# A second MLP product by Strassen: block sums and low parts of both operands on VectorE

## The reference

```python
a = jnp.square(jax.nn.relu(jnp.einsum('btd,df->btf', rmsnorm(h, ln2), w_ff1)))
return h + jnp.einsum('btf,fd->btd', a, w_ff2)
...
y_prompt = rmsnorm(yp, ln_f)
```

## Time and profile before

| | us |
|---|---|
| median of 3 runs | 1367.07 (1362.38 to 1369.3) |
| the profiled execution | 1365.83 |
| its span in the trace | 1363.9 |
| TensorE busy | 1287.0 (94%) |
| VectorE busy | 832.2 (61%) |
| GpSimd busy | 654.5 (48%) |
| ScalarE busy | 593.2 (43%) |

### The profile page before, as it was taken

One profiled execution on the slowest core, in us unless ns is written; L12 is line 12 of the kernel. 1 busy time (PEld: TensorE's weight loads), 2 busy tenths in 40 slices (PEclk: granted clock), 3 DMA queues, 4 the chain that ended last, 5 costly groups with the idle time before them and its releaser, 6 DMA issues.

```text
span 1363.9 us, 25942 instructions
## 1 busy us (share of the span) xinstructions
PE 1287.0 (94%) x10008; PEld 1190.0 (87%) x10008; DVE 832.2 (61%) x1678; ACT 593.2 (43%) x1099; POOL 654.5 (48%) x588
## 2 busy tenths in 40 slices
PE   5999999999998999999999999999979998986898
PEld 5859999995666899789999999999979998986798
DVE  6368997669874222148634334335578677598955
ACT  6445888638765223236443333334112323321334
POOL 5434984433312113121567667675448477385500
PEclk9999999999999999999999999999999998997899
DMA  6430124210011866871333233233801502402003
GB/s 191 94 85 16 48 55 126 82 29 1 2 32 56 301 207 202 287 236 36 115 117 112 90 115 116 89 111 143 297 1 42 210 1 94 158 1 94 32 1 127
DMA packets 140288, 141.72 MB, mean 104 GB/s; under 512 B 20888, under 2 KB 98840, under 8 KB 140159
## 3 DMA queue, kind: packets, MB, share of 16 engines
q1 hardware_dynamic: 121669, 116.31, 26.7%
q10 hardware_dynamic: 17842, 21.94, 4.5%
q0 software_dynamic: 656, 1.84, 0.6%
HBM read 111.87 MB, written 26.50 MB: 101 GB/s over the span
## 4 chain that ended last, share of the span: by engine, by line
PE 67%; DVE 13%; POOL 5%; issue 3%; ACT 2%; DMA 0%; SPq 0%; DVEq 0%; ACTq 0%; POOLq 0%
PE bank L2350 60%; POOL a L1057 3%; PE bank L2541 3%; DVE bo_lo L2177 3%; DVE b L2185 2%; PE bank L2640 2%; POOL ao_lo L1053 2%; DVE acc L2200 2%; DVE junk L1813 1%; DVE P_sum L2200 1%; PE bank L2595 1%; ACT sjunk L1226 1%; PE bank L2398 1%; ACT ao_hi L1536 1%; DVE acc L2216 1%
## 5 line engine op out<-in xcount | busy, mean ns | idle before, releaser
L2350 PE MATMUL bank<-bo_hi,ao_hi 128*128 128x264 f32 x672 | 196.8, 293 | 39.3 <-DVE bo_lo L2177 39.3
L2350 PE MATMUL bank<-bo_lo,ao_hi 128*128 128x264 f32 x672 | 195.1, 290 | 0.0
L2350 PE MATMUL bank<-bo_hi,ao_lo 128*128 128x264 f32 x672 | 195.0, 290 | 0.0
L777 POOL TENSOR_TENSOR w_hi<-w_raw,zero 128x256 fp32r<-128x256 f32 x108 | 68.2, 632 | 205.8 <-PE bank L2350 187.7
L2350 PEld LDWEIGHTS bank<-bo_hi,ao_hi 128*128 128x128 f32 x672 | 131.2, 195 | 40.8 <-DVE bo_lo L2177 40.8
L1053 POOL TENSOR_TENSOR ao_lo<-a,ao_hi 128x2048 fp32r<-128x2048 f32 x21 | 104.8, 4990 | 109.6 <-ACT ao_hi L1536 109.6
L2350 PE MATMUL bank<-xn_hi,w_hi 128*128 128x384 f32 (+1 forms) x456 | 150.6, 330 | 0.0
L2350 PE MATMUL bank<-xn_lo,w_hi 128*128 128x384 f32 (+1 forms) x456 | 147.3, 323 | 0.0
L2350 PE MATMUL bank<-xn_hi,w_lo 128*128 128x384 f32 (+1 forms) x456 | 146.9, 322 | 0.0
L2350 PEld LDWEIGHTS bank<-bo_lo,ao_hi 128*128 128x128 f32 x672 | 131.2, 195 | 0.0
L2350 PEld LDWEIGHTS bank<-bo_hi,ao_lo 128*128 128x128 f32 x672 | 131.1, 195 | 0.0
(11 more groups left out here) (322 smaller groups left out, 3565.4 us busy)
## 6 DMA issues: line engine op xcount, KB each, us to landing
page<-in_cache_k_dram SPq DMA_DIRECT2D x64, 256.0 KB, 3.6
page<-in_cache_v_dram SPq DMA_DIRECT2D x64, 256.0 KB, 3.4
hidden_dram<-stg ACTq DMA_DIRECT2D x56, 264.0 KB, 2.0
b<-hidden_dram SPq DMA_DIRECT2D x12, 1056.0 KB, 6.8
a<-in_w_ff_dram SPq DMA_DIRECT2D x12, 1024.0 KB, 8.6
w_raw<-in_w_ff_dram SPq DMA_DIRECT2D x22, 512.0 KB, 5.0
w_raw<-in_w_in_dram SPq DMA_DIRECT2D x18, 512.0 KB, 3.6
wr<-in_w_ff_dram SPq DMA_DIRECT2D x14, 512.0 KB, 4.6
```

The source lines that it names most:

```text
L777: nc.gpsimd.tensor_tensor(w_hi[n % 2][:, c], w_raw[n % 2][:, c], zero_w[:, 0:WP], ALU.add).then_inc(s_whi, 1)
L2350: return nc.tensor.matmul(out, lhsT, rhs, start=start, stop=stop)
```

## The change

Both operands' sums (S1 to S4, T1 to T4) and low parts are made by VectorE, in one order of jobs that is written out for each product: job j runs ahead of the addition of tile j. GpSimd has nothing left of the three groups. One semaphore counts all sums, one all low parts. ScalarE makes bo_hi ahead of ao_hi in P1, P2, P3, P7 and P4. The final combinations are placed anew: P2's between the additions of P6, P6's after P6, P3 - P5 after P7, and the last sixteen (`closing`) in the first eight tiles of the last stage. Some buffers of the last stage lie elsewhere, and GpSimd's memset of `ysq` comes earlier.

```diff
             for sg in range(1, SG):
                 stored_upto(FG + 2 * KH * (sg + 1))
-                sp.wait_ge(s_dbs, 4 * (sg - 1) + 2)
+                sp.wait_ge(*summed(sg - 1, "T2"))
                 b_load(sg, "b12")
-                sp.wait_ge(s_dal, q0 + 4)
+                sp.wait_ge(*lowed(sg - 1, "aP3"))
                 a_load(sg, "a12")
-                sp.wait_ge(s_dal, q0 + 5)
-                sp.wait_ge(s_das, 4 * (sg - 1) + 4)
+                sp.wait_ge(*lowed(sg - 1, "aP6"))
                 a_load(sg, "a21")
...
-            for sg in range(SG):
-                q0 = 7 * sg
-                a_low(q0, "a11")
-                a_low(q0 + 1, "a12")
...
-                a_sum("a21", "a21", "a22", ALU.add)
-                a_low(q0 + 2, "a21")
...
-                a_sum("a21", "a21", "a11", ALU.subtract)
-                a_sum("a12", "a12", "a21", ALU.subtract)
-                a_low(q0 + 3, "a12")
-                a_sum("a11", "a22", "a21", ALU.subtract)
-                a_low(q0 + 4, "a21")
-                a_low(q0 + 5, "a11")
-                a_low(q0 + 6, "a22")
...
-            pool.wait_ge(s_cf, NCF)
+            wait_full(pool, ("dn", 0, KC - 1, 2))
             nc.gpsimd.memset(ysq[:, T:NT * P], 0.0).then_inc(s_ypad, 1)
...
+                if name in ("P1", "P2", "P3", "P7", "P4"):
+                    values_high()
+                    weights_high()
                 else:
+                    weights_high()
+                    values_high()
...
+            work = {"P1": ("T1", "bP2", "aP2", "S1"), "P2": ("aP5", "bP5", "S2", "S4"), "P5": ("bP3", "T2", "aP3", "S3"),
+                    "P3": ("T3", "aP6", "bP6", "T4"), "P6": ("bP7", "aP7"), "P7": ("bP4", "aP4"), "P4": ("bP1", "aP1")}
             for q in range(NQ):
...
+                jobs = list(work[name])
                 for i in range(MP):
-                    if tail and name == "P4":
-                        combine_parts("P7", "P7", "P6", ALU.add, i)
-                        combine_parts("P4", "P4", "P7", ALU.add, i, combined[0])
-                        dve.wait_ge(s_cf, combined[0])
+                    job = jobs[i] if i < len(jobs) else None
+                    if job in D_SUMS:
+                        block_sum(sg, job)
+                    elif job and q + 1 < NQ:
+                        low(q + 1, job[0])
                     product_add(q, i)
+                    if tail and name == "P6":
+                        combine_parts("P2", "P2", "P1", ALU.add, i)
                     if tail and name == "P4":
                         last_low(i)
-                    if i == 1:
-                        if name == "P1":
-                            product_low(q + 1)
...
+                if tail and name == "P7":
+                    product_settled(q)
                     for i in range(MP):
+                        combine_parts("P3", "P3", "P5", ALU.subtract, i)
...
+            def closing(q):
+                i, n = q % MP, combined[0]
+                if q < MP:
+                    combine_parts("P7", "P7", "P6", ALU.add, i)
+                    combine_parts("P4", "P4", "P7", ALU.add, i, n + 1)
+                else:
+                    combine_parts("P3", "P3", "P6", ALU.add, i, n)
+                    combine_parts("P5", "P7", "P5", ALU.subtract, i, n)
...
                 nc.vector.tensor_tensor(v, ps[:, 0:w], v, ALU.add).then_inc(freeof(("last", q)), 1)
+                if q < 2 * MP:
+                    closing(q)
```

More of the change, by code:

```diff
@@ L75, in hymba_pool_dsa_step @@
     MP = KC // 2
-    NCF = 8 * MP
+    D_SUMS = {n: i + 1 for i, n in enumerate(("T1", "S1", "S2", "S4", "T2", "S3", "T3", "T4"))}
+    D_LOWS = {n: i + 1 for i, n in enumerate(("bP1", "aP1", "bP2", "aP2", "aP5", "bP5", "bP3", "aP3",
+                                             "aP6", "bP6", "bP7", "aP7", "bP4", "aP4"))}
     in_cols = ([QI0, QI0 + P, KI0] + [U0 + P * c for c in range(C4)] + [V0 + P * c for c in range(C4)]
@@ L1527, in product_high @@
                     wait_full(act, ("ds", q - 2, MP - 1, 1))
[L1528 to L1533, removed]
-                else:
-                    act.wait_ge(s_qa[a], Q_LOADED + 16 * (sg + 1))
@@ L1536, in product_high @@
[L1536 to L1541, removed]
+                a, a_sum = {"P1": ("a11", None), "P2": ("a12", None), "P5": ("a21", "S1"), "P3": ("a12", "S4"),
+                            "P6": ("a21", "S2"), "P7": ("a11", "S3"), "P4": ("a22", None)}[name]
@@ new lines, in product_high, with weights_high @@
+                b, b_sum = {"P1": ("b11", None), "P2": ("b21", None), "P5": ("b12", "T1"), "P3": ("b22", None),
+                            "P6": ("b22", "T2"), "P7": ("b11", "T3"), "P4": ("b21", "T4")}[name]
+                def weights_high():
+                    if a_sum:
+                        act.wait_ge(*summed(sg, a_sum))
+                    else:
+                        act.wait_ge(s_qa[a], Q_LOADED + 16 * (sg + 1))
+                    nc.scalar.activation(ao_hi[q % 2][:, :, :], a_q[a][:, :, :], ACT.Copy).then_inc(s_dah, 1)
@@ L2166, in last_low @@
             def last_low(k):
-                dve.wait_ge(s_dbl, NQ)
+                dve.wait_ge(*lowed(SG - 1, "bP4"))
                 dve.wait_ge(s_hh, FG + k + 1)
@@ L2171, in last_low, with low @@
                                         ALU.subtract).then_inc(s_fl, 1)
[L2173 to L2185, removed]
+            def low(q, side):
+                n = DPRODS[q % 7]
+                if side == "b":
+                    src = b_q[{"P1": "b11", "P2": "b21", "P5": "b12", "P3": "b22", "P6": "b22", "P7": "b11", "P4": "b21"}[n]]
+                    hi, dst = bo_hi[q % 2], bo_lo[q % 2]
+                    dve.wait_ge(s_dbh, q + 1)
+                else:
+                    src = a_q[{"P1": "a11", "P2": "a12", "P5": "a21", "P3": "a12", "P6": "a21", "P7": "a11", "P4": "a22"}[n]]
+                    hi, dst = ao_hi[q % 2], ao_lo[q % 2]
+                    dve.wait_ge(s_dah, q + 1)
+                nc.vector.tensor_tensor(dst[:, :, :], src[:, :, :], hi[:, :, :].bitcast(F), ALU.subtract).then_inc(s_dlow, 1)
@@ new lines, in block_sum @@
+            def block_sum(sg, n):
+                if n in ("S1", "T1"):
+                    for x in {"S1": ("a21", "a22"), "T1": ("b11", "b12")}[n]:
+                        dve.wait_ge((s_qa if n == "S1" else s_qb)[x], Q_LOADED + 16 * (sg + 1))
+                dst, x, y, op = {"T1": ("b12", "b11", "b12", ALU.subtract), "T2": ("b22", "b22", "b12", ALU.add),
+                                 "T3": ("b11", "b22", "b11", ALU.subtract), "T4": ("b21", "b21", "b22", ALU.subtract),
+                                 "S1": ("a21", "a21", "a22", ALU.add), "S2": ("a21", "a21", "a11", ALU.subtract),
+                                 "S4": ("a12", "a12", "a21", ALU.subtract), "S3": ("a11", "a22", "a21", ALU.subtract)}[n]
+                for w in {"T1": (), "S1": (), "S2": (lowed(sg, "aP5"), summed(sg, "S1")),
+                          "S4": (summed(sg, "S2"), lowed(sg, "aP2")), "T2": (lowed(sg, "bP3"), summed(sg, "T1")),
+                          "S3": (summed(sg, "S2"), lowed(sg, "aP1")), "T3": (summed(sg, "T2"), lowed(sg, "bP1")),
+                          "T4": (summed(sg, "T2"), lowed(sg, "bP2"))}[n]:
+                    dve.wait_ge(*w)
+                part = a_q if n[0] == "S" else b_q
+                nc.vector.tensor_tensor(part[dst][:, :, :], part[x][:, :, :], part[y][:, :, :], op).then_inc(s_dsum, 1)
@@ L2247, in _ @@
                 if m == 5:
-                    product_low(0)
+                    low(0, "b")
+                    low(0, "a")
                 for g in range(3):
```

97 lines of the change are left out of this document (37 added, 60 removed).

## The result

| | before | after |
|---|---|---|
| median | 1365.69 us (4 runs, 1362.38 to 1369.30) | 1319.28 us (4 runs, 1316.42 to 1320.78) |
| ratio | | 0.9657, 95% interval 0.9626 to 0.9689 |
| profiled execution, its span | 1365.83, 1363.9 | 1318.54, 1316.7 |
| first product to last stage | 299.25 | 251.88 |
| last stage to the end | 62.9 | 65.0 |

A forecast was written before the change was run, and what follows sets the result against it. TensorE was held by waits on VectorE's late low parts, slowed beside GpSimd, and by clock falls. 1001.72 + 244.9 + 2.8 + 3.5 started the last stage at 1252.9, 48.1 us earlier: 1319 us, range 1312 to 1337.

The forecast's parts named there:

- The cause: 21 products: VectorE's sums and low parts are slow only where GpSimd works, 6.67 us against 2.35, making bo_lo late.
- Rival 3: VectorE's jobs: slowness comes from ScalarE or the DMAs, jobs stay at 4.78 us, kernel slower at 1440; chance 0.04.
- The a jobs: 21 low parts and 12 sums of 128x2048 moved to VectorE: about 2.28 us each, started 2.20 apart.
- The schedule of a group: Seven undisturbed products: VectorE's jobs fit TensorE's 11.66 us each, no stall, tightest room 1.2 us before P6.
- Rival 1: Four-job products: VectorE becomes the bound; 0.15 us more a job gives 1323, 0.3 gives 1337; put at 1328, chance 0.20.
- The first group: First seven products: stalls of 1.2 us at P2, 1.5 at P3 and 0.1 at P6, sum 2.8.
- The clock: Among the 21 products: 12.0 us lost to clock falls behind five long waits, 2.4 us each, would be regained.
- The last wait: TensorE's wait on hl_lo ahead of the last stage: 3.5 us taken, between 1.9 and 4.9, against 3.1 before.
- Granted clock 1.00 throughout: Sign of the forecast: TensorE's granted clock stays at 1.00, 2.4 GHz, throughout.
- what follows it stays: From the start of the last stage on: time unchanged, only that start comes 48.1 us earlier.
- The closing work: 16 last combinations moved into tiles 0 to 7 of the last stage: taken as 0, 11.2 us if all exposed.
- rival 2: Last stage: the closing combinations are exposed, +11.2 us, 1330, with TensorE waiting for banks after tile 3; chance 0.05.

The follow-up runs named there:

- experiment 1: Kernel before, GpSimd's a-side sums and low parts replaced by memsets that read nothing: three memsets each 1344.04 us (0.9839), two and a half 1322.28 us (0.9666).
- weights first: Changed kernel with ScalarE's high part of the a side always ahead of the b side's, as before: 1336.14 us, ratio 0.9763.
- GpSimd waiting: Changed kernel with early hl_lo, combinations at head and tail moved, and GpSimd waiting for all hl_lo before its third and fourth wl_lo: 1312.78 us, ratio 0.9592.

## Why the prediction was right

- *The cause* (GpSimd's reads, not VectorE's own speed) was read from two rows of one instruction, 2.35 and 6.67 us. The run with the collision removed and nothing moved has a stage 45.4 us shorter, against 47.4 by the change. What the prediction did not separate is that half of this went over GpSimd's own jobs (experiment 1). Rival 3 is out: with GpSimd at rest no sum or low part took over 2.36 us.
- *The a jobs:* estimated at 2.28 us, 2.20 apart; measured 2.284, and 2.20 to the start of the next instruction.
- *The schedule of a group:* aP5 at 2.25, S4 at 13.2, bP6 at 10.5 were forecast, and 2.2, 13.2, 10.4 came. Rival 1 (0.3 us more a job) did not come.
- *The first group:* 1.2, 1.5 and 0.1 us forecast, 1.04, 1.16 and none measured.
- *The clock:* the 12.0 us of slow clock between products were given back to within 0.5 us (251.88 less 21 x 11.66 and 6.5 of waits); the two short waits, 1.04 and 1.16 us, did not make it fall.
- *The last wait:* 3.5 was a middle between 1.9 and 4.9, and 4.3 came, nearer the late end. The Trainium skill's page "SBUF — State Buffer", section "Who interferes with whom", says that a VectorE instruction with two SBUF inputs and a GpSimd instruction that reads SBUF contend. That was the ground for the late end, and the rows agree: 2.65 and 2.77 us for a low part that takes 1.24 alone.
- *Missed:* that the clock would fall behind the last wait. "Granted clock 1.00 throughout" was wrong there (0.50 from 1251 to 1256), and so was "what follows it stays", by 2.1 us. It did not show in the total, because the profiled execution reached the first product 1.9 us sooner (999.79 against 1001.72). That is not the change's doing: the same kernel, run again on another chip, reached it at 1001.50. 47.4 - 2.1 + 1.9 is the 47.2 by which the spans differ, against 48.1 forecast.
- *The closing work* was free as forecast (rival 2 out): no wait of TensorE in the last stage is on a bank, and without the fall of the clock that stage takes 62.8 us against 62.9 before. All the combinations in their old places cost 12 us of stage; how much of that is the closing work's alone was not run.

That the median hits the forecast to a fraction of a microsecond is partly luck. Two errors of 2 us cancel. The medians fell by 46.4 us, not 48.1, but the kernel before's, over four runs, is 1365.69 and not the 1367.07 that the forecast started from. And medians of the kernel before moved by 4 us from chip to chip.

## What to carry to other kernels

Before work is given to GpSimd to relieve VectorE, look for one VectorE form with two durations: if the long one stands only beside a GpSimd read of SBUF, the help costs both engines, and VectorE alone, though 85% busy, was faster here by 46 us. When the bulk is moved, look at the last GpSimd reads that stay: the last two of four still held the tail for 3.4 us when all else was mended, and a wait that let VectorE go first was worth as much as two rearrangements, some 4 us each. A schedule written out job by job from pitches (the time from one start to the next, not the duration) was good to 0.1 us in the second group and 0.4 in the first. It says in advance which order and which insertions the full products can't bear, though not always at what price: ScalarE's old order cost 14 to 17 us, not 6.

## What the runs showed of the hardware that was not expected

- The collision is not even. Beside 90 GpSimd additions VectorE's b sums grew from 2.35 to 2.81 us while GpSimd's took 2.64, against an estimated 1.6 by the rate of its larger ones. In the kernel before VectorE waited more: its b sums took 4.78 instead of 2.35 us, GpSimd's a sums 6.20 instead of 4.6. The same 20 products with memsets, 125 us of them, changed nothing (2349 ns).
- Whether a short wait of TensorE costs the clock is not a matter of its length alone: behind waits of 3.0 to 3.1 us the next five microseconds had 1.00 three times (the kernel before from 1300, two places of the run with a's low parts on GpSimd) and 0.66 once (the same run, from 1060). Behind 2.1 to 2.5 us they had 0.66 to 0.68 three times (a's low parts on GpSimd 2.13, weights first 2.24, combinations as before 2.53) and 1.00 once (weights first, 2.40). Behind 3.3 to 3.6 us they had 0.66 to 0.67, and behind every wait of 4.3 us and more 0.50 to 0.71. Up to 1.56 us it never fell.
- Four profiled executions (weights first, a's low parts on GpSimd, GpSimd waiting, GpSimd's added reads) show the clock at 0.86, 0.90, 0.90 and 0.90 from 300 to 350, in the attention stage, where the code is the same in all kernels and the others have 1.00. Their first products start at 1005.59, 1005.52, 1002.77 and 1003.40, the others' from 999.38 to 1002.24, so stages were compared from the first product on. What made the clock fall there stays open.
